# Attention in head pairs on halves of the array, norm chains with squares from the banks, three tiles abreast

## The reference

```
def rmsnorm(x, g):
    y = xf * lax.rsqrt(jnp.mean(xf * xf, axis=-1, keepdims=True) + NORM_EPS)
    return y * g

def grouped_attend(q, k, v):                  # branch C, and B for context tokens
    s = jnp.einsum('bngqd,bnkd->bngqk', q, k)
    p = jax.nn.softmax(s, axis=-1)
    return jnp.einsum('bngqk,bnkd->bngqd', p, v)

# branch B for latent tokens: s_loc = q k + bias inside a window, joined with the context scores
...
hl = modulate(rmsnorm(xl, norm_mix_pre[l]), mod_l[0], mod_l[1])
zl = hl @ w_in[l]
...
xl = xl + mod_l[2] * rmsnorm(m_l, norm_mix_post[l])
f_l = conv_ffn(modulate(rmsnorm(xl, norm_ffn_pre[l]), mod_l[3], mod_l[4]), ffn_up[l], ffn_conv[l], ffn_down[l])
xl = xl + mod_l[5] * rmsnorm(f_l, norm_ffn_post[l])
```

## Time and profile before

| | |
|---|---|
| time of the kernel, three runs | 2069.81 us median (2069.78 to 2072.62) |
| the profiled execution | 2068.46 us, span of its instructions 2066.7 us |
| PE busy | 1908.6 us (92%), weight loads 1567.8 us |
| DVE, ACT, POOL busy | 988.2, 820.6, 283.9 us |
| mean granted TensorE clock | 0.964 |

### The profile page before, as it was taken

One profiled execution on the slowest core, in us unless ns is written; L12 is line 12 of the kernel. 1 busy time (PEld: TensorE's weight loads), 2 busy tenths in 40 slices (PEclk: granted clock), 3 DMA queues, 4 the chain that ended last, 5 costly groups with the idle time before them and its releaser, 6 DMA issues. The chain is left out here.

```text
span 2066.7 us, 28022 instructions
## 1 busy us (share of the span) xinstructions
PE 1908.6 (92%) x11608; PEld 1567.8 (76%) x11608; DVE 988.2 (48%) x1555; ACT 820.6 (40%) x1306; POOL 283.9 (14%) x227
## 2 busy tenths in 40 slices
PE   4899998989999999799999996999897989989997
PEld 1688557959877777478888883875685979979997
DVE  1353437456333333455554215544746636557763
ACT  2421455152242223544343226325516234366553
POOL 1040432021000000011221001304202000002211
PEclk9899999989999999899999997999998999989999
DMA  8632642020343222213232336533102045434554
GB/s 246 211 99 82 195 145 82 1 79 4 91 155 102 82 82 82 82 63 121 82 102 77 93 116 170 192 125 113 62 1 62 1 143 176 151 122 157 191 160 127
DMA packets 225645, 228.64 MB, mean 111 GB/s; under 512 B 5168, under 2 KB 214320, under 8 KB 225392
## 3 DMA queue, kind: packets, MB, share of 16 engines
q1 hardware_dynamic: 210560, 190.40, 29.2%
q0 software_dynamic: 14960, 36.44, 6.1%
HBM read 214.24 MB, written 12.58 MB: 110 GB/s over the span
## 5 line engine op out<-in xcount | busy, mean ns | idle before, releaser
L752 ACT ACTIVATE whi<-ring 128x1024 fp32r<-128x1024 f32 (+1 forms) x264 | 275.3, 1045 | 707.6 <-PE ps L1505 643.5
L1077 DVE TENSOR_TENSOR wlo<-ring,whi 128x1024 fp32r<-128x1024 f32 (+1 forms) x264 | 319.3, 1213 | 213.2 <-ACT whi L752 212.5
L1503 PE MATMUL ps<-H,whi 128*128 128x512 f32 (+1 forms) x704 | 240.9, 342 | 13.9 <-DVE H L1116 13.5
L1504 PE MATMUL ps<-H,whi 128*128 128x512 f32 (+1 forms) x704 | 238.8, 339 | 0.0
L1505 PE MATMUL ps<-H,wlo 128*128 128x512 f32 (+1 forms) x704 | 238.6, 339 | 0.0
L1503 PE MATMUL ps<-HG,whi 128*128 128x512 f32 (+1 forms) x512 | 191.1, 373 | 0.8 <-DVE wlo L1077 0.7
L1505 PE MATMUL ps<-HG,wlo 128*128 128x512 f32 (+1 forms) x512 | 172.7, 337 | 0.0
L1504 PE MATMUL ps<-HG,whi 128*128 128x512 f32 (+1 forms) x512 | 172.2, 336 | 0.0
L1503 PE MATMUL ps<-HR,whi 128*128 128x512 f32 (+1 forms) x384 | 144.0, 375 | 22.8 <-DVE HR L1116 22.8
L1503 PEld LDWEIGHTS ps<-H,whi 128*128 128x128 f32 x704 | 135.2, 192 | 32.6 <-issue 13.8
L1505 PEld LDWEIGHTS ps<-H,wlo 128*128 128x128 f32 x704 | 135.6, 193 | 13.9
(11 more groups left out here) (285 smaller groups left out, 3535.6 us busy)
## 6 DMA issues: line engine op xcount, KB each, us to landing
ring<-in_ada_w SPq DMA_DIRECT2D x48, 1024.0 KB, 5.3
ring<-in_ffn_up SPq DMA_DIRECT2D x44, 1024.0 KB, 5.1
ring<-in_w_gate SPq DMA_DIRECT2D x32, 1024.0 KB, 5.4
ring<-in_w_in SPq DMA_DIRECT2D x24, 1024.0 KB, 5.2
ring<-in_ffn_down SPq DMA_DIRECT2D x32, 512.0 KB, 3.8
WB<-in_w_branch POOLq DMA_DIRECT2D x8, 1024.0 KB, 6.6
ring<-in_w_o SPq DMA_DIRECT2D x8, 1024.0 KB, 5.3
ring<-in_ffn_down SPq DMA_DIRECT2D x16, 384.0 KB, 3.7
```

What stands on the lines that cost most here:

```text
L752: act.activation(whi[:, m % SPLIT, 0:kn, :], ring[:, SLOT[raw] % RING, 0:kn, P * half:P * half + P], ACT.Copy).then_inc(hi_done, 1)
L1077: dve.tensor_tensor(wlo[:, m % SPLIT, 0:kn, :], ring[:, SLOT[raw] % RING, 0:kn, P * half:P * half + P], whi[:, m % SPLIT, 0:kn, :].bitcast ...
L1503: pe.matmul(o[:, c0:c1], hi[:, i, :], part(0, k), start=(k == 0), stop=False)
L1504: pe.matmul(o[:, c0:c1], hi[:, i, :], part(1, k), start=False, stop=False)
```

## The change

There are three parts.

**Attention.** Units are taken in pairs of heads that lie on different halves of the partitions (`HEAD_PAIRS`). The score matmuls of a pair read only their 64 rows, so `KZ` and its DVE work go. PV of a pair alternates between the two column halves. All loops now go by pairs `j = 0, 2, 4, ...`, and `pr`, `prT` and `sbuf2` have four buffers in place of three.

**Norms.** For k = 1 and k = 3 ACT squares the tile from the bank, before it copies it; DVE adds squares 1 to 6 into square 0 (`sum_square`), and PE makes two matmuls in place of eight. ACT loads one table set (`ROOT_TABLE`) ahead of the projection whose results are squared.

**Three abreast.** `project_first` runs the first three tiles of z and of up together over the first five contraction tiles, then finishes each.

```
+HEAD_PAIRS = {"B": ((0, 1), (2, 3)), "C": ((0, 3), (1, 2))}
+ROOT_TABLE = "natural_log_exp_and_others"
+ABREAST = 5
...
-    return [(g, h, q) for g in "BC" for h in range(HEADS) for q in tiles]
+    return [(g, h, q) for g in "BC" for pair in HEAD_PAIRS[g] for q in tiles for h in pair]
...
@@ DVE @@
-                for i in range(len(units) + 3):
-                    if i < len(units):
...
-                    if 1 <= i <= len(units):
-                        u = i - 1
-                        emptied(dve, ("S", l, u))
-                        dve.reciprocal(stat[:, 2, u % 4:u % 4 + 1], stat[:, 1, u % 4:u % 4 + 1]).then_inc(p_sum, 1)
+                for j in range(0, len(units) + 4, 2):
+                    if j < len(units):
+                        for i in (j, j + 1):
...
+                    if 2 <= j <= len(units):
+                        for u in (j - 2, j - 1):
+                            emptied(dve, ("S", l, u))
+                            dve.reciprocal(stat[:, 2, u % 4:u % 4 + 1], stat[:, 1, u % 4:u % 4 + 1]).then_inc(p_sum, 1)
...
@@ PE @@
-                pe.wait_ge(kz_ready, 6 * l + 6)
...
+                for j in range(0, len(units) + 4, 2):
+                    if j < len(units):
+                        for i in (j, j + 1):
...
+                            tq, tk = (Z_NQ + h // 2, Z_NK + h // 2) if g == "B" else (Z_GQ + h % 2, Z_GK)
+                            x = HD * (h % 2 if g == "B" else h // 2)
+                            o = job(("S", l, i))
+                            done(pe.matmul(o[:, 0:nk], Z[x:x + HD, tq, 128 * q:128 * q + 128], Z[x:x + HD, tk, 0:nk],
+                                           start=True, stop=True))
+                    fill(("att", l, j))
+                    if 2 <= j <= len(units):
+                        for u in (j - 2, j - 1):
...
+                            pe.wait_ge(p_ready, UBASE[l] + u + 1)
...
+                    if j >= 4:
+                        outs = [job(("PV", l, u), u - j + 4) for u in (j - 4, j - 3)]
...
+                        for b in range(nt):
+                            for o, u in zip(outs, (j - 4, j - 3)):
...
+                                last = pe.matmul(o[half, 0:128], v, prT[:, u % 4, 128 * b:128 * b + 128],
+                                                 start=(b == 0), stop=(b == nt - 1))
...
@@ ACT, after the output projection (k = 1) and after down (k = 3) @@
+                act.preload_act_table_set(ROOT_TABLE)
                 for j in range(KT):
                     s = filled(act, ("wo", l, j))
-                    split_until(min(half_no(("wo", l, j)) + 1 + SPLIT, half_no(("up", l, 0, 0)) + SPLIT))
+                    if j < KT - 1:
+                        split_until(min(half_no(("wo", l, j)) + 1 + SPLIT, half_no(("up", l, 0, 0)) + SPLIT))
+                    square(SQB[:, j, c0:c1], s[:, c0:c1])
                     act.activation(OB[:, j, c0:c1], s[:, c0:c1], ACT.Copy).then_inc(frees(("wo", l, j)), 1)
-                    emptied(act, ("wo", l, j))
-                    square(SQB[:, j, c0:c1], OB[:, j, c0:c1])
+                split_until(half_no(("up", l, 0, 0)) + SPLIT)
...
@@ DVE @@
+                def sum_square(k, SQ, j):
...
+                    dve.tensor_tensor(SQ[:, 0, c0:c1], SQ[:, 0, c0:c1], SQ[:, j, c0:c1], ALU.add).then_inc(sq_summed, 1)
...
@@ PE @@
-                for i in range(KT):
+                if k % 2:
+                    pe.wait_ge(sq_summed, (KT - 2) * (2 * l + k // 2 + 1))
+                for i in (0, KT - 1) if k % 2 else range(KT):
...
+            def project_first(names, part, cs, made):
...
+                order = [(k, n) for k in range(ABREAST) for n in range(len(names))]
+                order += [(k, n) for n in range(len(names)) for k in range(ABREAST, KT)]
+                for k, n in order:
...
+                    if n == 0:
+                        pe.wait_ge(made[0], made[1] + k + 1)
+                    pe.matmul(o, hi[:, k, :], part(0, k)[:, c0:c1], start=(k == 0), stop=False)
+                    pe.matmul(o, hi[:, k, :], part(1, k)[:, c0:c1], start=False, stop=False)
+                    last = pe.matmul(o, lo[:, k, :], part(0, k)[:, c0:c1], start=False, stop=(k == KT - 1))
```

More of the change, by code:

```diff
@@ L179, in job_list @@
         n = len(attention_units(l))
-        for i in range(n + 3):
+        for i in range(0, n + 4, 2):
             if i < n:
-                jobs.append(("S", l, i))
+                jobs += [("S", l, i), ("S", l, i + 1)]
             jobs += FILL.get(("att", l, i), [])
[L184 to L187, removed]
+            if 2 <= i <= n:
+                jobs += [("T", l, i - 2), ("T", l, i - 1)]
+            if i >= 4:
+                jobs += [("PV", l, i - 4), ("PV", l, i - 3)]
         for d in range(2):
@@ L454, in build @@
         sq_ready = sem("sq_ready")
+        sq_summed = sem("sq_summed")
         h_full = sem("h_full")
@@ L841, in _ @@
                 act.wait_ge(h_saved[l], 32)
-                for i in range(len(units) + 2):
-                    if i < len(units):
[L844 to L858, removed]
+                for j in range(0, len(units) + 2, 2):
+                    if j < len(units):
+                        for i in (j, j + 1):
+                            g, h, q = units[i]
+                            nk = T if q >= 2 else CTX
+                            s = bank(("S", l, i))
+                            src = sbuf2[:, i % 4, 0:nk] if g == "B" and q >= 2 else s[:, 0:nk]
+                            act.wait_ge(nmax_ready, UBASE[l] + i + 1)
+                            act.activation(pr[:, i % 4, 0:nk], src, ACT.Exp, bias=stat[:, 0, i % 4:i % 4 + 1],
+                                           accum_out=stat[:, 1, i % 4:i % 4 + 1]).then_inc(frees(("S", l, i)), 1)
+                    fill(("att", l, j))
+                    if j >= 2:
+                        for u in (j - 2, j - 1):
+                            nk = T if units[u][2] >= 2 else CTX
+                            s = filled(act, ("T", l, u))
+                            if u >= 4:
+                                act.wait_ge(mm_done, JOB[("PV", l, u - 4)] + 1)
+                            act.activation(prT[:, u % 4, 0:nk], s[:, 0:nk], ACT.Copy).then_inc(frees(("T", l, u)), 1)
                 act.wait_ge(ya_ready, 2 * l + 2)
@@ L1051, in _ @@
                         split_until(half_no(("down", l, j)) + 6)
+                    square(SQF[:, j, c0:c1], s[:, c0:c1])
                     act.activation(F[:, j, c0:c1], s[:, c0:c1], ACT.Copy).then_inc(frees(("down", l, j)), 1)
-                    emptied(act, ("down", l, j))
-                    square(SQF[:, j, c0:c1], F[:, j, c0:c1])
                 norm_root(l, 3)
@@ L1214, in _ @@
                             dve.tensor_scalar(v, v, HD ** -0.5, None, ALU.mult).then_inc(q_scaled, 1)
[L1215 to L1225, removed]
@@ L1447, in _ @@
                 product_lo(FT - 1)
-                split_until(half_no(("down", l, 0)) + 3 * KT)
+                for j in range(KT):
+                    split_until(half_no(("down", l, 0)) + min(3 * j + 6, 3 * KT))
+                    if 0 < j < KT - 1:
+                        sum_square(3, SQF, j)
                 for j in range(KT):
@@ L1510, in project @@
                 done(last)
+            def project_first(names, part, cs, made):
+                outs = [job(name, n) for n, name in enumerate(names)]
+                tiles = []
+                for name in names:
+                    tiles += halves(name)
+                order = [(k, n) for k in range(ABREAST) for n in range(len(names))]
+                order += [(k, n) for n in range(len(names)) for k in range(ABREAST, KT)]
+                for k, n in order:
+                    c0, c1 = cs[n]
+                    o, (hi, lo) = outs[n][:, c0:c1], tiles[n]
+                    if n == 0:
[3 more added lines that the diff above has]
+                    last = pe.matmul(o, lo[:, k, :], part(0, k)[:, c0:c1], start=False, stop=(k == KT - 1))
+                    if k == KT - 1:
+                        done(last)
             def fill(point):
@@ L1561, in _ @@
                 pe.wait_ge(qk_ready, 3 * l + 3)
-                pe.wait_ge(kz_ready, 6 * l + 6)
+                for p in range(2):
+                    emptied(pe, ("z", l, Z_NK + p))
                 for i in range(3):
```

128 lines of the change are left out of this document (63 added, 65 removed).

## The result

The changed kernel takes 2096.4 us (median of 4, 2095.1 to 2100.1) against 2071.2 us for the kernel before beside it: a ratio of 1.0126, with a 95% interval of 1.0111 to 1.0141. It is slower by some 26 us. Ratios here are of fast executions alone: one of the five of the kernel with the tiles abreast alone was slow, with 6567 us, and without it that kernel's median is 2060.7 us.

What follows compares the result with a forecast made beforehand. PE was taken to bound the kernel, busy for 92% of the span. 23 + 21 - 14.3 - 12 = +18 on the span of 2066.7 gave 2085, as a time 2087 us; range 2064 to 2108.

Steps and rivals of the forecast that it cites:

- The likeliest case: Whole kernel: PE waits in attention, with the clock down half the time, +6 to +30 us; chance 0.53.
- Attention at full clock: Both attention stages: each pair step becomes a serial chain over PE, DVE and POOL, 103 and 66 us, +23 us.
- The clock in attention: Attention: PE's clock falls to half in the gaps, 43 us if cold throughout, 0 if never; half taken, +21 us.
- PE busy near half: Sign in the attention windows: PE busy for about half of some 115 and 75 us.
- Norm chains: Norm roots of both layers: shorter sums and fewer table loads gain 7.1 + 3.7 + 3.5 = 14.3 us.
- Root 1 of layer 0: Norm chain there: ACT's own tail decides and Ln and Exp go without the load, 5.8 us gained.
- Root 0: Norm chain of layer 1: two loads leave the path and modulation matmuls run sooner; 3.5 us gained, ends 0 and 5.5.
- Three abreast: First three tiles of z and up: PE busy from the start, gains 3.0, 2.6, 5 and 1.5, together 12 us.
- B (clock holds): Rival: PEclk stays above 0.9 in attention, -3 us, about 2067 us; chance 0.19.
- D (cold nearly throughout): Rival: clock down for nearly all of attention, +39 us, about 2108 us; chance 0.13.
- E: Rival: column halves don't overlap, PV of a pair costs 0.87 or 0.44 us more, about 2104 us; chance 0.08.
- C, attention that gets faster: Rival: T finds its row ready, steps of about 4.6 us against 6.6, about 2004 us; chance 0.07.

## Why the prediction was right, and where its numbers were off

The forecast was 2087 us, by waits in attention and a clock that is down for part of it, and the time is 2096. The likeliest case came about, by its own mechanism, at the upper end of its range (2076 to 2100).

- **Attention at full clock, +23 us: right.** With the clock held up the stages took 103.5 and 66.6 us against the forecast 103 and 66, a step of B 8.95 against 4.19 + 3.12 + 0.1 + 0.53 + 1.02 = 8.96, and one of C 7.38 against 2.7 + 3.12 + 0.1 + 0.53 + 1.02 = 7.47. The chain was read from the earlier trace rows alone.
- **The clock in attention, +21 us: right in kind, measured 24.5.** PEclk was 0.77 and 0.74, inside 0.6 to 0.9; by that mean (2 x (1 - 0.77) x 117, and so on) the clock was at half for about 54 of 117 and 40 of 77 us, near the half that was assumed. The half was a choice between two ends and no result, so its closeness is in part luck. "PE busy near half" was wrong: it is busy for 75% and 67%, since at half clock the same work takes longer and fills part of the gap (140.2 us in the two stages, against 100.6 for the same instructions at PEclk 1.00 with T a pair later). That is also the likely reason that T waits 52.6 us for POOL and not over 60.
- **The clock behind attention: left out.** The recurrent stages brought +1.8 and +4.1 us. I had no term for where the clock falls in other stages; the runs spread by 3 and 6.5 us there.
- **Norm chains, 14.3 us: right**, 13.5 in the changed kernel and 14.4 alone. Root 1 of layer 0 was forecast at 5.8 and gave 6.04 (9.83 to 3.79), all of layer 0 7.1 and 7.3, layer 1 3.7 and 4.0. Root 0 gave 2.2 and not 3.5. Its modulation matmuls did run sooner, but the z weight blocks that were asked for sooner did not land sooner, as ACT's order at root 0 of the changed kernel shows:

```profile
1280.26 1.06 ACT L753 ACTIVATE whi<-ring 128x1024 fp32r<-128x1024 f32 x1 [0.67 <-DMA ring<-in_w_in]
1281.22 0.67 ACT L732 ACTIVATE rt<-ps,eps 128x512 f32<-128x512 f32 x1
1281.92 0.63 ACT L735 ACTIVATE rs<-rt 128x512 f32<-128x512 f32 x1
```

  Ln stands behind the split of a block that lands 27.7 us after the start of root 3 (1252.58 to 1280.26), 27.1 before the change. What is left is the two loads, 2.56, less that half microsecond. The median from issue to landing of these blocks rose from 17.2 to 22.9 us beside the reload of X.
- **Three abreast, 12 us: right**, 12.4 by stages and 10 alone. z of layer 1 gave 6.6 and not 5 (13.41 us, not 15), up of layer 0 only 1.8 over its stage.
- **Rivals.** B (clock holds) falls with PEclk of 0.77 and 0.74. D (cold nearly throughout) falls with the same values. E falls with 16 product records in 1.09 us. C, attention that gets faster, was excluded rightly for this order, but it is real: 2004 us and steps of about 4.6 were its price, and 2011 and 4.55 are what one pair more of distance gives. The Trainium skill (TensorEngine Tiling (Array Packing), Theoretical Speedup) gives up to 2x where a dimension is 64 or less; the traces agree and stay somewhat below it, with factors of 1.8 (1.91 to 1.06) for row halves and 1.85 (1.89 to 1.02) for column halves.

The terms summed to +17.7 on the span and the difference is +28.1. The missing 10.4 are 4.6 from attention (3.5 of it clock), 5.9 from the recurrent stages and 0.8 from the norms, less 0.4 for the tiles abreast and 0.4 ahead of the first of them. The step that failed most is thus one that was not there: a term for the clock outside attention. How much of it this change brings is not shown, since the recurrent stage of layer 1 took 6.1 us more with the attention of before as well.

## What to carry to other kernels

Where work is merged into larger steps, count the distance between producer and consumer in steps again: here one unit of lag, enough at 2.5 us a unit, became none, and that alone cost 24 us at full clock. Write down the loop over all engines for one step; if it holds an instruction of each and is longer than the bound engine's own work, either move the early one forward or the late one back. And where PE must wait, price the wait twice: once as idle time and once at the lower clock of the work behind it, which here cost as much again.

## What the runs showed of the hardware that was not expected

- Matmuls without use, put into a gap, paid for themselves: 252 more records in the attention of layer 0 (921 against 669), PEclk from 0.77 to 0.98, the stage from 117.1 to 103.5 us.
- Row halves and column halves both overlap nearly fully for f32 here, also where the pair's two score matmuls write different banks: 1.06 us for 4 records of 512 columns that take 1.91 on the same half.
- The recurrent stage of layer 1 differs by up to 6.5 us (394.6 to 401.1) between kernels that issue the same instructions there, with PEclk of 0.95 to 0.97.
